# Two-layer hybrid block, second attention: block-head pairs interleaved with differential pairs

## What is computed

```
(mq, mk, mv, dq, dk, dv, sq, sk, sv, iq, ik, iw) = split(rms_norm(x) @ w_in)
moba = softmax(causal(q k)) v          # 4 heads of 64; all past blocks are kept at 512 positions
diff = (softmax(q1 k1) - lam * softmax(q2 k2)) v     # 4 heads, v is 128 wide
diff = rms_norm(diff, diff_subln_g) * (1 - lam_init)
dsa  = softmax over the 128 best keys of each query, by an index score   # 4 heads of 64
x    = x + concat(moba, diff, dsa) @ w_out
```

## Time and profile before

| | us |
|---|---|
| median of the runs | 2879.3 |
| the profiled execution | 2879.06 |
| its span, first to last instruction | 2877.3 |
| one "attn2" stage, each of two layers | about 105 |
| PE / DVE / ACT / POOL busy in one stage | 92.1 / 78.0 / 62.2 / 4.0 |

### The profile page before, as it was taken

How to read it: one execution, slowest core, us unless ns; L and a number is a source line. 1 busy time by engine, 2 the same in 40 slices (tenths; PEclk the granted TensorE clock), 3 DMA queues, 4 the chain that set the end, 5 groups by cost and what they waited for, 6 DMA issues and landing times. The chain is left out here.

```text
span 2877.3 us, 33717 instructions
## 1 busy us (share of the span) xinstructions
PE 2532.5 (88%) x12728; PEld 2079.0 (72%) x12728; DVE 1492.3 (52%) x2510; ACT 1214.4 (42%) x2420; POOL 654.1 (23%) x348
## 2 busy tenths in 40 slices
PE   6989796966989886974998889999979988899998
PEld 6877675756877675754786768888876867788886
DVE  1845647853745657845498642232215986333222
ACT  3436626743436625752464632222136446222211
POOL 3400404753400314762351000000023601000000
PEclk9989987987989987995998899999979989999999
DMA  4110017953210017953220022222211201122221
GB/s 145 56 48 1 1 60 298 359 216 117 66 48 1 1 60 275 357 212 115 73 88 30 1 83 105 88 94 89 85 59 59 90 14 48 64 88 97 94 83 64
DMA packets 53792, 282.97 MB, mean 98 GB/s; under 512 B 13056, under 2 KB 13056, under 8 KB 27008
## 3 DMA queue, kind: packets, MB, share of 16 engines
q1 hardware_dynamic: 44416, 264.03, 25.6%
q0 software_dynamic: 9216, 16.80, 1.5%
HBM read 274.49 MB, written 23.07 MB: 103 GB/s over the span
## 5 line engine op out<-in xcount | busy, mean ns | idle before, releaser
L185 ACT ACTIVATE weights_hi<-weights_raw 128x2048 fp32r<-128x2048 f32 (+5 forms) x138 | 240.9, 1745 | 682.6 <-PE ps L208 618.5
L195 POOL TENSOR_TENSOR weights_lo<-weights_raw,weights_hi 128x2048 fp32r<-128x2048 f32 (+5 forms) x60 | 262.0, 4367 | 849.3 <-ACT weights_hi L185 807.6
L195 DVE TENSOR_TENSOR weights_lo<-weights_raw,weights_hi 128x2048 fp32r<-128x2048 f32 (+3 forms) x78 | 165.5, 2122 | 534.0 <-ACT weights_hi L185 534.0
L206 PE MATMUL ps<-y2t_hi,weights_hi 128*128 128x512 f32 x704 | 280.5, 398 | 10.2 <-PEq L1605 10.2
L208 PE MATMUL ps<-y2t_hi,weights_lo 128*128 128x512 f32 x704 | 280.5, 398 | 0.0
L207 PE MATMUL ps<-y2t_lo,weights_hi 128*128 128x512 f32 x704 | 278.1, 395 | 0.0
L206 PE MATMUL ps<-weights_hi,attn_ht_hi 128*128 128x512 f32 (+2 forms) x576 | 216.5, 376 | 4.9 <-PEq L229 4.9
L207 PE MATMUL ps<-weights_lo,attn_ht_hi 128*128 128x512 f32 (+2 forms) x576 | 213.2, 370 | 0.0
L208 PE MATMUL ps<-weights_hi,attn_ht_lo 128*128 128x512 f32 (+2 forms) x576 | 212.7, 369 | 0.0
L206 PEld LDWEIGHTS ps<-y2t_hi,weights_hi 128*128 128x128 f32 x704 | 133.2, 189 | 42.1 <-DVE weights_lo L195 10.9
L207 PEld LDWEIGHTS ps<-y2t_lo,weights_hi 128*128 128x128 f32 x704 | 133.3, 189 | 33.4
(11 more groups left out here) (461 smaller groups left out, 5875.0 us busy)
## 6 DMA issues: line engine op xcount, KB each, us to landing
weights_raw<-in_stream SPq DMA_DIRECT2D x108, 1024.0 KB, 4.8
weights_raw<-in_expert_gu SPq DMA_DIRECT2D x34, 1024.0 KB, 9.1
expert_raw<-in_expert_gu SPq DMA_DIRECT2D x30, 1024.0 KB
expert_raw<-in_expert_down SPq DMA_DIRECT2D x18, 1024.0 KB, 8.1
weights_raw<-in_expert_down SPq DMA_DIRECT2D x14, 1024.0 KB, 8.4
weights_raw<-in_stream SPq DMA_DIRECT2D x12, 960.0 KB, 4.6
ln_more<-expert_rows SPq DMA_DIRECT2D x16, 512.0 KB, 6.8
weights_raw<-in_stream SPq DMA_DIRECT2D x8, 700.0 KB, 12.9
```

The costliest lines, as they stand in the source:

```text
L185: self.nc.scalar.activation(self.split_tiles(u)[0][:, 0:n], self.env.raw[:, u % self.RAW, 0:n], ACT.Copy).then_inc(self.hi_ready, 1)
L195: eng.tensor_tensor(lo[:, 0:n], self.env.raw[:, u % self.RAW, 0:n], hi[:, 0:n].bitcast(F32), ALU.subtract).then_inc(self.lo_ready, 1)
L206: nc.tensor.matmul(out, a[0], b[0], start=start, stop=False, **more)
```

## The change

```diff
 class DiffEnd:
-    NH, W, FIRST = 4, 128, 20
+    NH, W = 4, 128

-    def __init__(self, env, ctx, y):
-        self.env, self.y = env, y
+    def __init__(self, env, ctx, y, units):
+        self.env, self.y, self.units, self.FIRST = env, y, units, units + 3
...
         if t == 0:
-            act.wait_ge(out_stored, self.NH * T)
+            act.wait_ge(out_stored, self.units)
...
-                diff_end = DiffEnd(env, heads, proj[:, :, B_DQ:B_DQ + 512])
+                diff, moba = iter(pairs[0:4 * T]), iter(pairs[4 * T:6 * T])
+                pairs = [next(kind) for _ in range(2 * T) for kind in (moba, diff, diff)] + pairs[6 * T:]
+                diff_end = DiffEnd(env, heads, proj[:, :, B_DQ:B_DQ + 512], 6 * T)
```

## The result

The changed kernel takes 2895.55 us (median of 20 runs, 2893.74 to 2906.25) against 2881.99 us for the kernel before (20 runs, 2876.07 to 2897.14). The ratio is 1.0046, with a 95% interval of 1.0036 to 1.0055: slower by about 13 us, 0.5%, where 6 us less had been forecast.

What follows compares the result with a forecast made beforehand. DVE was taken to set the pace first, then PE. Per layer -3.5 - 1.1 + 1.6 = -3.0 us, for two layers -6.0, from the profiled 2879.06 us to 2873 us; range 2866 to 2885.

Steps and rivals of the forecast that it cites:

- Root and table load in step 31: Between the last exponentials and unit 30's copies: lengthens the chain to the last output by 1.6 us per layer.
- Units 0 to 23: Reordered units: DVE's waits for scores shrink from 6.5 to 3.0 us, a gain of 3.5 us per layer.
- Units 24 to 27: Behind unit 24's maximum: less leftover PE work, unit 27's maximum at 8.5 instead of 9.6 us, gaining 1.1 per layer.
- Squares: ACT in steps 27 to 30: four squares per step, 1.17 us, covered beside PE's work; counted as nothing.
- POOL: Behind the root at the stage's end: 4.04 us of work, just covered by 0.6 us before the last output.
- Table loads that go: Exponentials' table reload and one load in the next stage disappear; both stood beside PE work, so nothing gained.
- The one that went to the slower side: First 24 units: clock falls among M units too, five falls of 2.3 us per layer; 2890 us, chance 0.12.
- a PEclk below 0.80 over the first 24 units: First 24 units: PE's granted clock under the 0.80 they have now would decide for the slower rival.
- The rival in which the waits only move: First 24 units: DVE and PE stay coupled, 6.4 us of waits remain, +0.5 per layer; 2880 us, chance 0.18.

Runs made afterwards that it cites:

- s3_fill: Changed kernel plus 8 more PE matmuls of 128x512 in step 32, during the tail's wait for the copies; 2887.87 us, ratio to before 1.0027.
- t1: s6 plus 3 to 6 more matmuls where PE waits for VectorE among the first 24 units; 2867.89 us, ratio to before 0.9954.
- t2: Kernel before, order unchanged, plus filling matmuls where PE waits among the D units; 2874.7 us, ratio to before 0.9962.
- r1_after_again: The changed kernel run and profiled once more, unaltered; 2896.01 us, ratio to before 1.0062.
- s6: Changed kernel with squares taken one by one as units are stored, root and table load in step 28; 2882.6 us, ratio to before 1.0006.
- s2_old_no_end: Kernel before (old order) without the end of the differential heads (squares, root, inversion, POOL's products); 2882.4 us, ratio to before 1.0009.
- s1: Changed kernel (new order) without the end of the differential heads (squares, root, inversion, POOL's products); 2881.58 us, ratio to before 1.0006.
- r3: Changed kernel with a scaled copy in place of the root, so no table load in step 31; 2884.07 us, ratio to before 1.0018.

## Why the prediction was wrong, step by step

Three terms failed, all by what PE's clock does behind a pause. Per layer, the root and table load were priced 3.7 us too low, units 24 to 27 came out 2.6 us above the forecast on average, and units 0 to 23 2.5 us above it. The first is the largest and the one that experiments isolate.

**Root and table load in step 31: the step that failed.** The forecast priced them at +1.6 us, "on the chain copies, transposes, values, last output". The mechanism and the 1.6 us were right; s3_fill shows 9.4 us against 7.8. What was left out is that PE stands still meanwhile, and that the work behind it then runs at the 1.2 GHz level: another 3.7 us per layer. I had seen the pattern in the D units, where a fall of the clock stood behind a pause of 1.05 us, and applied it only there. A wait of 2.0 us, in a stage whose last 4.1 us are nothing but PE work, was the plainest place for it. The term should have been +5.3.

**Units 0 to 23, forecast -3.5 us.** The amount of DVE work was about right: less its waits for scores, the stretch takes 67.9 us in t1 and 68.4 in t2 (layer 1), where the forecast had 68.9. What it had wrong is the falls of the clock, in number and in cost. I took "two or three falls per layer instead of four", each with waits of 1.0 to 1.2 us. I cut the traces into slices of 0.4 us and call a fall a run of slices with a granted clock near 0.5. The six stages in the old order without filling have four falls each in the first 24 units. The fourteen in the new order without filling have three (five stages) or four (nine). And a fall costs more there. In layer 1 of r1_after_again three of them make DVE wait 2.2, 3.0 and 2.5 us; these two waits are those of the second, from 1583.7 to 1590.5:

```profile
1585.82 0.42 DVE L2560 TENSOR_REDUCE attn_top<-ps 128x2 f32<-128x256 f32 x1 [1.16 <-PE ps L2521]
...
1589.75 0.69 DVE L2560 TENSOR_REDUCE attn_top<-ps 128x2 f32<-128x512 f32 x1 [1.85 <-PE ps L2521]
```

The granted clock over the stretch is 0.82 to 0.88 in the fourteen stages and 0.80 to 0.84 in the six. The fourteen take 74.3 us on average (71.6 to 75.5), the six 75.4 (74.0 to 76.3): a gain of about 1 us. The first profile's 71.6 us in layer 1 came close to the forecast 71.8, by luck. It has three falls, one of them short.

The other half of the idea, that mixed units balance DVE and PE, holds where the clock does. The old order keeps 2.7 us of waits at full clock, all among the M units (t2). The new order has in t1 only 0.2 us outside the one fall that makes DVE wait; without that fall its stretch would take about 68 us instead of t2's 71.1, an estimate from 71.1 less 1.60 and 1.44. No run has the new order without any fall.

**Units 24 to 27, forecast -1.1 us.** At full clock it is just that: 8.6 us in t1, against the 8.5 I had stepped out and the 9.6 of before. But the new order puts the last D3 step, the longest on DVE, directly ahead, so that PE pauses 1.32 us, and the clock falls in units 24 to 27 in all fourteen stages. M3's values still run nearly at full pace, the next scores do not:

```profile
1636.47 1.97 PE L2547 MATMUL ps<-proj,attn_prob_t 128*128 128x64 f32 x16 [1.32 <-DVE proj L2578]
1638.37 1.04 PE L2518 MATMUL ps<-qk_t 64*128 64x256 f32 x4
```

At full clock the values took 1.90 us and the scores 0.70. In t1, with six more matmuls in that pause, the fall is gone. Measured: +0.6 to +2.1 us, +1.5 on average. From the first maximum to that of unit 27 the new order takes 85.4 us on average and the old 85.0, so the reordering gains nothing by unit 27 as it stands.

**Squares, forecast nothing.** 27 to 31 takes 11.8 us in every run that has four squares in each of these steps and 11.4 in those that have none or have them earlier: +0.4 us per layer. In s6 and t1, with the last squares, root and load there, it is 11.6. **POOL, forecast covered by 0.6 us:** covered, by 4.3 us, since the tail grew. **Table loads that go:** nothing, as forecast; s2_old_no_end, which has fewer, is not faster.

Summed per layer: +5.3 + 0.4 for the end, -1.0 for the first 24 units and +0.6 to +2.1 behind them, together 5.3 to 6.8 us, and 0.2 to 0.5 more in the next stage, 11 to 15 us for two layers; measured 13.6 by the medians.

**The rivals.** The one that went to the slower side had the right cause, PE's pauses halving the clock, and about the right price for a fall, 2.3 us. Its sign, a PEclk below 0.80 over the first 24 units, did not come, and it placed the whole loss there, while most of it came in the tail. The page beside it, the Trainium skill, "TensorE: Matmul & The Clock Gate", section on psum-queue depth-cycling, says that brief frequent idling makes the clock swing; the filled runs agree (granted clock 1.00 instead of 0.80 in t2), and the chance of 0.12 that I gave this rival was too low. The rival in which the waits only move is what the reordering alone does (s1 against s2). The page beside that one, the Trainium skill, "Perfetto Trace Analysis", section Identifying the Most-Contended Engine, led by its weight-load measure to DVE as the most contended engine in both stretches; t2 speaks against that for the M units, where DVE waits 2.7 us for PE at a granted clock of 1.00.

**What stays open.** Each profile is one draw of where the clock falls; how often each order draws which falls over many executions was not measured. Why the next stage's transposes run at full clock in six of the runs is not shown. Of the 7 us between t1 and t2, the stages show some 2 us (0.8 and 1.0 us in the two layers behind unit 24); the rest may be scatter between the runs. Other amounts of filling were not tried, which might remove t1's last falls, nor the filling of the tail together with t1.

## What to carry to other kernels

Where a wait is put on the path of TensorE, price it twice: its length, and the work behind it at half clock, here 1.6 us and 3.7 us. Before instructions are moved toward the end of a stage, ask what still stands beside them there; a root with its table load that cost nothing among other units cost 5.3 us in the last ones. And where TensorE pauses while another engine sets the pace, a few matmuls that nobody needs may be faster than none: here they gave 7 to 11 us in the kernel before, and 15 in one whose new order had by itself given nothing.

## What the runs showed of the hardware that was not expected

Added work made the kernel faster: 48 more matmuls in the old order's first 24 units took the granted clock there from 0.80 to 1.00 and the stretch from 75.3 to 71.1 us. A pause of 2.0 us on PE was enough to put all that was left of the stage at the 1.2 GHz level, which turned 4.1 us of PE work into 7.8 us. And the same program draws its falls of the clock differently from execution to execution: the changed kernel's first 24 units took 71.6, 73.8, 75.5 and 75.5 us in two profiles, and the code ahead of the first attention stage, which no experiment altered, took 16.3 us more in the profile of after than in that of before, 13.0 more in r3's and 22.7 more in t2's, so that a stage has to be compared from its own first instruction.
